# Weight slabs at other distances from their inputs, and a short opening product, in a two-block float32 forward pass

## What is computed

```python
def hybrid_layer(x, norm_w, w_in, w_out, ...):
    h = rmsnorm(x, norm_w)
    p = split_cols(h @ w_in)
    ...                       # four mixers: two attentions, a short convolution, a pooling
    return x + mixed @ w_out
```

```python
for l in range(2):
    xl = post_norm(xl, 0.5 * g1 * swiglu(modulate(xl, ...), ffn1_w_in[l], ffn1_w_out[l]))
    xc = post_norm(xc, 0.5 * cg1 * swiglu(modulate(xc, ...), ffn1_w_in[l], ffn1_w_out[l]))
    ...                       # l = 0: gated linear and latent attention; l = 1: neighbourhood attention
    xl = post_norm(xl, g2 * yl)
    xl = post_norm(xl, 0.5 * g3 * swiglu(modulate(xl, ...), ffn2_w_in[l], ffn2_w_out[l]))
```

## Time and profile before

| what | us |
|---|---|
| median of 3 runs (2055.27 to 2055.6) | 2055.31 |
| the profiled execution, whole | 2058.96 |
| its span, first to last instruction | 2057.1 |
| TensorE busy in the span, 12728 matmuls | 2029.4 |
| VectorE busy | 1371.3 |
| ScalarE busy | 754.6 |

### The profile page before, as it was taken

How to read it: one execution, slowest core, us unless ns; L and a number is a source line. 1 busy time by engine, 2 the same in 40 slices (tenths; PEclk the granted TensorE clock), 3 DMA queues, 4 the chain that set the end, 5 groups by cost and what they waited for, 6 DMA issues and landing times. The chain is left out here.

```text
span 2057.1 us, 30253 instructions
## 1 busy us (share of the span) xinstructions
PE 2029.4 (99%) x12728; PEld 1762.6 (86%) x12728; DVE 1371.3 (67%) x2147; ACT 754.6 (37%) x936; POOL 154.1 (7%) x138
## 2 busy tenths in 40 slices
PE   9999999999999999999999999999999999999998
PEld 8979979888888988688888888888888899779998
DVE  6966975776785667657876775655455465567555
ACT  4464465222213544435222222521212242565333
POOL 0410500000002000020000003000000210010001
PEclk9999999999999999999999999999999999999999
DMA  6653654554543210223454543332532343114552
GB/s 242 227 173 140 242 182 156 188 198 166 204 159 120 114 44 9 105 82 132 180 191 174 194 173 124 123 141 93 196 133 98 118 165 141 55 61 152 188 174 103
DMA packets 68768, 301.39 MB, mean 147 GB/s; under 512 B 6176, under 2 KB 23200, under 8 KB 48672
## 3 DMA queue, kind: packets, MB, share of 16 engines
q1 hardware_dynamic: 65920, 290.06, 39.0%
q10 hardware_dynamic: 2720, 9.51, 1.3%
HBM read 298.50 MB, written 1.05 MB: 146 GB/s over the span
## 5 line engine op out<-in xcount | busy, mean ns | idle before, releaser
L482 PE MATMUL PS<-xh,wh 128*128 128x512 f32 (+1 forms) x3676 | 1000.8, 347 | 2.5 <-DVE wh L398 1.0
L482 PEld LDWEIGHTS PS<-xh,wh 128*128 128x128 f32 x3676 | 659.0, 188 | 91.9 <-issue 1.7
L482 PE MATMUL PS<-xl,wh 128*128 128x512 f32 (+1 forms) x2086 | 706.4, 339 | 0.0
L394 ACT ACTIVATE wh<-raw 128x2048 fp32r<-128x2048 f32 (+4 forms) x221 | 377.6, 1710 | 301.3 <-PE PS L482 227.6
L398 DVE TENSOR_TENSOR wh<-raw,wh 128x2048 fp32r<-128x2048 f32 (+3 forms) x183 | 376.2, 2056 | 101.8 <-ACT wh L394 101.4
L482 PEld LDWEIGHTS PS<-xl,wh 128*128 128x128 f32 x2086 | 391.9, 188 | 43.9
L482 PE MATMUL PS<-HH,wh 128*128 128x512 f32 (+1 forms) x1276 | 347.8, 359 | 0.1
L1349 DVE CUSTOM_DVE_ANT_0 NRM<-SQ,CBR 128x1024 f32<-128x1024 f32 x240 | 284.0, 1221 | 5.8
L1270 ACT ACTIVATE SI<-PS 128x512 f32<-128x512 f32 (+1 forms) x88 | 47.9, 544 | 584.1 <-PE PS L482 569.7
L482 PEld LDWEIGHTS PS<-HH,wh 128*128 128x128 f32 x1276 | 227.3, 188 | 37.2 <-DVE wh L398 0.9
L482 PE MATMUL PS<-HL,wh 128*128 128x512 f32 (+1 forms) x638 | 228.6, 358 | 0.0
(11 more groups left out here) (416 smaller groups left out, 2376.9 us busy)
## 6 DMA issues: line engine op xcount, KB each, us to landing
raw<-ffi_dram SPq DMA_DIRECT2D x88, 1024.0 KB, 4.9
SQ<-adat_dram SPq DMA_DIRECT2D x120, 512.0 KB, 3.4
raw<-ffo_dram SPq DMA_DIRECT2D x64, 704.0 KB, 4.2
raw<-layer_dram SPq DMA_DIRECT2D x36, 1024.0 KB, 5.0
lent<-layer_dram SPq DMA_DIRECT2D x14, 1024.0 KB, 7.3
raw<-odd_dram SPq DMA_DIRECT2D x12, 1024.0 KB, 4.8
raw<-even_dram SPq DMA_DIRECT2D x9, 1024.0 KB, 4.8
raw<-eout_dram SPq DMA_DIRECT2D x4, 1024.0 KB, 4.9
```

The source lines that it names most:

```text
L394: act.activation(high(i)[:, 0:n], raw[:, i.slot, 0:n], ACT.Copy).then_inc(hi_done, 1)
L482: m = pe.matmul(out, w[rows, o:o + P], x, start=n == 0 and j == 0, stop=n == len(tiles) - 1 and j == 2)
```

## The change

The high parts of nine slabs of the first layer start at places of their own (their low parts stay at 16). In the last stage both parts of nine slabs of `ffi210`, of eight slabs of `ffi211` (two at their old place) and of the eight slabs of `ffo210` do. In the second layer of the first block eight dense slabs get one extra matmul ahead of their own: the first weight tile against the first 16, 32, 64 or 128 columns of `xh`, into the bank that the slab's own first matmul then starts anew.

```diff
+    for k, at in zip((3, 4, 5, 8, 9, 10, 11, 12, 14), (24, 32, 48, 64, 80, 96, 8, 0, 40)):
+        hi[PLAN.index(("in", k))] = at
+    for k, at in enumerate((8, 16, 24, 32, 48, 64, 80, 96, 112)):
+        hi[START["ffi210"] + 2 + k] = lo[START["ffi210"] + 2 + k] = at
+    for k, at in enumerate((0, 8, 4, 12)):
+        for b in (START["ffi211"] + k, START["ffi211"] + 4 + k):
+            hi[b] = lo[b] = at
+    for k, at in enumerate((8, 16, 24, 32, 48, 64, 96, 112)):
+        hi[START["ffo210"] + k] = lo[START["ffo210"] + k] = at
     return hi, lo
+
+
+def first_columns():
+
+
+    s0 = START["layer1"]
+    return {s0 + PLAN.index(("in", k)): n for k, n in ((3, 32), (4, 64), (5, 128), (8, 16), (9, 32), (10, 64), (11, 128), (12, 16))}
+
+
+LEAD_COLS = first_columns()
...
         def dense_one(pe, i, chunks=2, ready=None):
 
             slab_begin(pe, i)
+            if i.base in LEAD_COLS:
+                n = LEAD_COLS[i.base]
+                pe.matmul(PS[:, i.par, 0:n], high(i)[:, 0:P], xh[:, 0, 0:n], start=True, stop=True)
             for c in range(chunks):
                 m = product(pe, PS[:, i.par, c * T:(c + 1) * T], i,
                             [((c * KT + k) * P, xh[:, k, 0:T], xl[:, k, 0:T]) for k in range(KT)], ready=None if c else ready)
```

## The result

| | median us | runs | profiled execution, its span |
|---|---|---|---|
| before | 2055.6 | 5 (2055.27 to 2056.18) | 2058.96, 2057.1 |
| with the change | 2062.27 | 5 (2061.44 to 2063.77) | 2061.44, 2059.6 |

The changed kernel takes 1.0031 of the time before, 95% interval 1.0019 to 1.0043: slower by 6.7 us. The two profiled executions differ by 2.5 us only. In a later session, beside the kernel before on one chip, the ratio is 1.0014 (1.0005 to 1.0023); what is known of the rest of the 6.7 us comes back under "Why".

The account below looks back on a forecast made before the run. TensorE bounds the kernel: number of matmuls times their spacing, a close pace of 113.3 ns or a wide one of 117.8. The terms summed to +0.34 us on 2055.31, about 2055.7 us, range 2051 to 2063.

Parts of the forecast that it names:

- the likeliest case: Whole kernel: paces drawn anew, prices inside the close and wide pace; +0.34 us, about 2055.7 us, chance 0.52.
- the first rival: Every moved slab: distances off 16 make the two reads collide, 0.12 us a matmul; +6.9, 2062.2 us, chance 0.22.
- The starting point: Profiled execution, 2058.96 us: its 3.65 us over the median is profiling cost, so the change is added to 2055.31.
- (a): Second layer: eight extra matmuls cost one weight load each, 0.11 us whether 16 or 128 columns; +0.88 us.
- (b): Second layer's eight opened slabs: each short matmul is a break, pace drawn anew at even odds; -0.64 us.
- (c): First layer's nine slabs with moved high parts: all taken as wide, where eight were; +0.21 us.
- (d): ffi210, nine slabs, two wide and seven close before: even odds after the move; +0.53 us.
- (e): ffi211, eleven slabs, all wide before: changes of distance may set paces anew for moved and unmoved; -1.17 us.
- (f): ffo210, eight slabs of 33 matmuls, all close: seven at even odds, the last hidden by a wait; +0.53 us.
- "Distance does nothing": Whole kernel: paces follow breaks alone, extra matmuls paid without return; +0.88, 2056.2 us, chance 0.18.
- "Everything settles close": Moved and opened slabs: distances off 16 may avoid what makes the pace wide; -5.1, 2050.2 us, chance 0.08.
- The bound of the chances: Whole kernel: about 0.2%, 4.1 us, can't be told from no change; faster 0.09, same 0.71, slower 0.20.

Follow-up runs that it names:

- the kernel at distance 32: Against the kernel before: all 25 slabs that the change moves in the last stage put at distance 32, nothing else; 2062.01 us, ratio 1.0016.
- the two heads in each layer: Against the kernel before: no slab moved, one extra short matmul ahead of in 3 and in 8 of both first-block layers; 2055.98 us, ratio 0.9990.

## Why the prediction was right in its range and wrong in its mechanism

The median came out at 2062.27 where I had said 2055.7. The range held it, by its upper end; the likeliest case did not. The case that fits is the first rival, but that its 2062.2 meets the 2062.27 is luck: it forecast +6.9 us, and beside the kernel before on one chip the change costs 2.8 (2061.56 against 2058.79), within the 0.2% that the prediction held for what can't be told from no change.

**The starting point.** The prediction called the 3.65 us of the profiled execution over the median the cost of profiling. No run bears that out: the profiled execution of the changed kernel is the fastest of its five (2061.44), and that with the openers alone is under its median (2057.16 against 2058.16). In the later sessions the kernel before has medians of 2058.6 to 2058.8, so 2055.31 was a low start for the sum.

**(a), the openers' cost: right.** An opener costs what the prediction took for one weight load, 0.11 us. This is in 9 of the changed kernel's second layer, 32 columns (start, us):

```profile
221.27 0.18 PE L612 MATMUL PS<-xh,wh 128*128 128x32 f32 x1
221.30 0.36 PE L501 MATMUL PS<-xh,wh 128*128 128x256 f32 x1
221.50 0.28 PE L501 MATMUL PS<-xl,wh 128*128 128x256 f32 x1
221.62 0.28 PE L501 MATMUL PS<-xh,rest 128*128 128x256 f32 x1
```

The slab's first matmul comes 0.03 us after it and the second 0.20 later, so the second is 0.11 us later than in a plain slab, where it comes 0.12 behind the start. Whole opened slabs, in 9 to in 11, say the same:

```profile
221.27:227.03 5.76, 5.76 (x51) 1.00 0.81 269
227.03:232.79 5.76, 5.76 (x51) 1.00 1.01 355
232.79:238.38 5.59, 5.59 (x52) 1.00 1.05 375
```

5.76 is the wide 5.65 and 0.11, with 32 and with 64 columns; 5.59 the close 5.44 and 0.15, with 128. Eight of them are 0.9 us, as the sum had it.

**(b), the pace drawn anew: right in size, wrong in kind.** Here is the stretch from the second layer's slab in 1 to in 13, which holds all eight openers, in before and in the changed kernel:

```profile
173.68:247.41 73.73, 73.73 (x631) 1.00 0.61 215
173.10:247.13 74.03, 74.03 (x638) 1.00 0.61 214
```

(a) and (b) together are +0.30 us, and I had +0.24. But the pace at a start isn't at even odds, with an opener or without. Where nothing was moved or put in, in 8 is wide in 20 of 20 places of the fourteen traces, in 5 close in 21 of 21 and in 15 close in 28 of 28; only some starts vary. In all three traces with the change's openers the opened slabs have the same paces: in 3, 5, 8 and 11 close, in 4, 9, 10 and 12 wide. At the head of a stream, behind a short product, in 3 and in 8 turn from wide to close; in a running stream the openers of 16 to 64 columns leave it wide or make it so, those of 128 turn it over. So in 4 and in 9, behind a close slab, are wide again by their own openers. That half of the eight came out close is how their column counts fall.

**(c), the first layer: near enough.** All nine are wide in the first trace, those at 64 and 0 at 117.8 ns, in 3, 5 and 11 a little above (118.8 to 118.9). The nine take 0.36 us more than before, 0.25 of it in 5; I had +0.21. In the trace of the change on the second chip in 5, at 48, is close and they take 0.12 more. The part alone has the ratio 0.9997.

**(d), (e), (f), the last stage: here the prediction failed.** It said that "with both parts moved together no row favours either pace, so even odds". For ffi210 that gave +0.53, for ffi211 -1.17, for ffo210 +0.53: -0.11 in all. The changed kernel's stages stand against the first trace of before, as the sum was made, at +1.60, -0.47 and +1.08: +2.2. Against the mean of the six traces at distance 16 in the table above, 142.18, the whole stands at +3.2; the last stage alone made the median 3.15 longer (2061.77 against 2058.62), a ratio of 1.0014. The step's premise fell, not its arithmetic: either pace can stand at 16, 48, 80 and 112 alone. The change gives 48, 80 or 112 to six of the 25 slabs in its loops and leaves two at 16; the other seventeen were close in no trace and ran from 0.5 ns under the wide pace to 2.3 over it, and the six came out wide behind them in the change's order. For seventeen slabs a draw became a cost that the place sets.

A part of (e) failed by itself. I had counted on ffi211 to gain 1.17 us because its eleven slabs were wide in the one trace I had the earlier trace rows. In three of the six traces at distance 16 they are close without any change, so half of that gain was there before. One trace's draw was taken for the kernel's.

**The first rival** had place and price nearly right. Its upper row, 0.12 us a matmul, which I took for the third spacing of a start, happens to be the highest that any slab held: 28.80 / 240 = 120.0 ns. What it had wrong is that every place pays: four of them don't, and the first layer, which it charged as well, costs nothing that can be measured. **"Distance does nothing"** is ruled out by the kernel at distance 32, 1.0016 (1.0007 to 1.0025), and by its twelve slabs at 120.0 ns, which no slab of the stage had in before. The rule of the Trainium skill, "TensorE: Matmul & The Clock Gate", section "Step-by-step: what each phase is for", that moving operand and weight load have ports of their own, therefore does not tell all: with identical instructions, columns and clock the spacing is 113.3 to 120.0 ns, by where the slab starts within 512 bytes, the activations staying where they are. That the two reads meet in the same place of memory would explain it; no run here looked at that, and it isn't shown. **"Everything settles close"** had one grain: a stream can be made close, by an opener of the right size and not by distance.

**What is left of 6.7 us.** The change again, on another chip, is 3 us slower than before, and its last stage alone is as well (2061.77 against 2058.62). The changed kernel has nearly the same median in both sessions, 2062.27 and 2061.56; it is before that moved, from 2055.6 to 2058.6 and more. Its five executions in the first session lie within 0.9 us, while 27 in the next one spread from 2054.73 to 2063.82. Of the 69 later executions of before only five are as low as those, so five in a row are hardly chance: something of that session or its chip held before low. What it was is open, as no trace of those five was kept; 11 or more executions of both on that chip would tell whether it lasts. A second, smaller part is a stretch at half clock. 752 to 762 us in the changed kernel, and under it the same matmuls from 745 to 770 us, in before and in the changed kernel:

```profile
752.00:762.00 10.00, 10.00 (x61) 8.62 (x61) 9.86 (x14) 7.41 (x8) 0.00 (x0) 0.83 0.14 39
...
745.11:770.09 24.98, 24.98 (x201) 1.00 0.10 33
744.88:771.06 26.18, 26.18 (x201) 0.93 0.10 31
```

A granted clock of 0.83 over 10 us is 3.4 us at 1.2 GHz instead of 2.4. TensorE was busy for 52.00 of the 52 us ahead of 752, at a clock of 1.00. The stretch costs the changed kernel 1.2 us in its trace. It stands in eight of the fourteen traces, among them that of the two heads in each layer, the fastest of all, and not in that of distance 32, so it doesn't go with the change's places; the trace with the first layer's places has a second one, at 290.6 us. I had expected none with the last stage's places alone, as that stage comes later, and that trace has it too. Neither trace of before has it. Of the 69 executions of before in the three sessions 15 have a mean clock of 0.998 (2059.8 us in the mean), 43 one of 0.999 (2058.3) and 10 one of 1.0 (2058.0). In the traces 0.998 stands only with the stretch, 0.999 with it and without it, so I take it for a cost that either kernel may meet; what brings it isn't known. In the first session all five of the changed kernel had 0.998.

**The bound of the chances.** I held 0.2% for what can be told from no change. The kernel before spreads by 9 us, 0.4%, from one execution to the next; the paces of the last stage alone account for up to 3.8 of it (140.83 to 144.66). With 11 executions against 21 or 27 the intervals here are 1.9 us to either side, so an effect of 3 us needs about that many, and the times of one execution of each can't show it.

## What to carry to other kernels

Where small matmuls run back to back and TensorE is the bound, measure the spacing per matmul from slab to slab, in several traces, before arguing from one: two values may both belong to the program. Then try the starts of stationary and moving operand an odd multiple of 16 float32 numbers apart, modulo 128: with 256 moving columns, and the activations at 112, slabs at 0, 32, 64 and in-between distances never reached the close pace here. Whether the distance counts or the place of the slab alone was not tested, and 512 columns at distance 0 lost nothing (226.7 ns, twice 113.3). A pace that is wide in every trace can be turned by one short matmul at the head of its stream, at 0.11 us, but only if nothing ahead of it varies.

## What the hardware showed that I had not expected

- One stream of 128x128 by 128x256 float32 matmuls has not one spacing but at least four, each exact to 0.1 ns over dozens of matmuls: 113.3, 117.3 to 117.8, 118.7 and 120.0 ns. With 512 columns it is 226.7.
- The same stage of the same program has different paces in different executions: ffi211 took 62.28 and 62.29 us in the two traces of before and 59.95 to 59.96 in three kernels that leave it as it is. What decides at its start wasn't found.
- A matmul of 128 columns, 0.06 us before the next, turned the pace of a running dense stream of 256 columns over, in both directions, in twelve of the fourteen places in the traces where one stands. The two where it did not are in 14 of both layers, only 24 matmuls behind the start of the stream.
- Behind a slab at distance 28 the next one, at 16, is close in six of six places in the three traces with the change's last stage; in the trace with the reversed distances it is once wide and once close.
